# Layer norm ahead of a feed-forward block: GpSimd's eight residual products are held until VectorE has corrected the first results, and ScalarE's copies of them are spread over the block

## The reference

```python
def layer_norm(x, g, b):
    mu = jnp.mean(x32, axis=-1, keepdims=True)
    var = jnp.mean(jnp.square(x32 - mu), axis=-1, keepdims=True)
    return ((x32 - mu) * lax.rsqrt(var + LN_EPS) * g + b)

def swiglu(h, w_gate, w_up, w_down):
    return (jax.nn.silu(h @ w_gate) * (h @ w_up)) @ w_down

for i in range(2):
    ...
    x = layer_norm(ALPHA * x + (1.0 + g_m) * y, ln_mix_g[i], ln_mix_b[i])
    h = x * (1.0 + sc_f) + sh_f
    y = swiglu(h, w_gate[i], w_up[i], w_down[i])
    x = layer_norm(ALPHA * x + (1.0 + g_f) * y, ln_ffn_g[i], ln_ffn_b[i])
```

## Time and profile before

| | us |
|---|---|
| median of 3 runs (lowest, highest) | 1160.9 (1159.54, 1163.73) |
| the profiled execution, whole | 1165.62 |
| its span, first to last instruction | 1164.3 |
| TensorE busy | 1132.3 (97%) |
| VectorE busy | 839.1 (72%) |
| ScalarE busy | 628.7 (54%) |
| GpSimd busy | 77.8 (7%) |

### The profile page before, as it was taken

The page is one execution under the profiler, slowest core; times in us unless marked ns, Lnnn a source line. Parts: engine busy times, 40 slices in busy tenths (PEclk is TensorE's granted clock), DMA queues, the critical chain, the costliest instruction groups (busy, mean ns, idle before and its releaser), DMA issues.

```text
span 1164.3 us, 24996 instructions
## 1 busy us (share of the span) xinstructions
PE 1132.3 (97%) x10542; PEld 1083.9 (93%) x10542; DVE 839.1 (72%) x1427; ACT 628.7 (54%) x1075; POOL 77.8 (7%) x101
## 2 busy tenths in 40 slices
PE   7999989999999999989999999999999999999998
PEld 6997779999998999989999999999999999999987
DVE  5699579888885788797566569768656667676743
ACT  3477447444443677666444454744654557565542
POOL 3000012000000200120000004400000000000000
PEclk9999999999999999999999999999999999999999
DMA  9963756988997544546646552754245554656550
GB/s 321 378 222 125 274 182 218 310 300 273 341 304 262 199 146 146 182 146 216 217 152 208 186 181 73 236 164 147 74 146 182 178 179 132 200 177 204 183 179 37
DMA packets 194687, 232.22 MB, mean 199 GB/s; under 512 B 4083, under 2 KB 169555, under 8 KB 194576
## 3 DMA queue, kind: packets, MB, share of 16 engines
q1 hardware_dynamic: 193984, 230.32, 59.5%
q0 software_dynamic: 592, 0.31, 0.2%
HBM read 229.56 MB, written 1.05 MB: 198 GB/s over the span
## 4 chain that ended last, share of the span: by engine, by line
PE 85%; DVE 8%; DMA 2%; issue 2%; ACT 1%; SPq 1%; POOL 0%; DVEq 0%; ACTq 0%
PE ps L154 84%; DVE wlo L187 2%; DMA raw<-in_w_in_even_dram 2%; PE ps L157 2%; DVE hL L196 1%; DVE T L187 1%; DMA MW<-in_w_mod_dram 1%; SPq L224 1%; DVE first L187 1%; DVE LT L196 1%; DVE LT L187 1%; DVE Fg L196 0%; ACT whi L166 0%; DVE T L196 0%; POOL T L187 0%
## 5 line engine op out<-in xcount | busy, mean ns | idle before, releaser
L187 DVE TENSOR_TENSOR wlo<-raw,whi 128x1024 fp32r<-128x1024 f32 (+1 forms) x346 | 408.7, 1202 | 165.4 <-ACT whi L166 163.0
L154 PE MATMUL ps<-hH,whi 128*128 128x256 f32 (+3 forms) x1792 | 516.9, 288 | 1.5 <-DVE hL L196 1.1
L154 PE MATMUL ps<-hH,wlo 128*128 128x256 f32 (+3 forms) x1792 | 505.8, 282 | 6.1 <-DVE wlo L187 6.1
L154 PE MATMUL ps<-hL,whi 128*128 128x256 f32 (+3 forms) x1792 | 505.7, 282 | 0.0
L166 ACT ACTIVATE whi<-raw 128x1024 fp32r<-128x1024 f32 (+1 forms) x346 | 349.8, 1033 | 198.9 <-PE ps L154 136.5
L154 PEld LDWEIGHTS ps<-hH,whi 128*128 128x128 f32 x1792 | 338.8, 189 | 7.2 <-issue 3.8
L154 PEld LDWEIGHTS ps<-hH,wlo 128*128 128x128 f32 x1792 | 338.9, 189 | 7.1 <-DVE wlo L187 7.1
L154 PEld LDWEIGHTS ps<-hL,whi 128*128 128x128 f32 x1792 | 339.3, 189 | 0.3
L154 PE MATMUL ps<-uL,whi 128*128 128x256 f32 x352 | 99.2, 282 | 0.0
L154 PE MATMUL ps<-uH,whi 128*128 128x256 f32 x352 | 99.0, 281 | 0.0
L154 PE MATMUL ps<-uH,wlo 128*128 128x256 f32 x352 | 98.4, 279 | 0.0
(11 more groups left out here) (314 smaller groups left out, 1618.3 us busy)
## 6 DMA issues: line engine op xcount, KB each, us to landing
MW<-in_w_mod_dram SPq DMA_DIRECT2D x47, 1024.0 KB, 6.3
raw<-in_w_up_dram SPq DMA_DIRECT2D x44, 1024.0 KB, 5.6
raw<-in_w_in_dram SPq DMA_DIRECT2D x36, 1024.0 KB, 5.0
raw<-in_w_down_dram SPq DMA_DIRECT2D x27, 1024.0 KB, 5.8
raw<-in_w_gate_dram SPq DMA_DIRECT2D x22, 1024.0 KB, 7.2
raw<-in_w_in_odd_dram SPq DMA_DIRECT2D x12, 1024.0 KB, 5.4
raw<-in_w_in_even_dram SPq DMA_DIRECT2D x8, 1024.0 KB, 9.6
raw<-in_w_down_dram SPq DMA_DIRECT2D x8, 768.0 KB, 6.9
```

Source lines behind the costliest of these rows:

```text
L154: return self.queued(self.e.matmul(out, lhsT, rhs, start=start, stop=stop, skip_group_check=True, **kw), length if pos is None else max(le ...
L187: return self.queued(self.e.tensor_tensor(out, a, b, op), 0.07 + cols(out) / self.RATE)
```

## The change

GpSimd gets a second wait, for `k.raw_done`, ahead of its eight products, where the norm is one that runs ahead of a feed-forward block (`early` with `to`). Each product and its copy are now emitted at least 2 us of modelled TensorE time after the one before. `gated` waits for less: steps 0 and 1 for `raw_done` alone, step 2 also for the last `hL`, step 3 also for the last copy to XA. Steps 2 and 3 swap their pieces of `LT`, so that the piece with `rstd` is used last.

```diff
@@ layer_norm @@
     k.hold = False
+    if early and to is not None:
+        while k.raw_done is None:
+            yield None
+        pool.wait_ge(*k.raw_done)
     for i in range(0, KD, 2):
         if to is not None:
             for j in (i, i + 1):
+                if early:
+                    yield k.pe.clock + 2.0
                 t = pool.tt(T(j), T(j), rstd, ALU.mult).inc()
                 yield due(t)
                 new[j] = act.wait_ge(*t).act(X(j), T(j), ACT.Identity, scale=ag[:, j:j + 1], bias=ab[:, j:j + 1]).inc()
@@ gated @@
-    sg = m.l4[s % 4]
+    sg = m.l4[(0, 1, 3, 2)[s % 4]]
     if s == 0:
         f = m.first
         c = yield from normalized(k, y, f)
-    while not k.normed or k.raw_done is None:
+    while k.raw_done is None or s == 3 and not k.normed:
         yield None
     yield due(y, k.raw_done)
     act.wait_ge(*y)
     if s == 0:
         act.table(SET_SILU)
     if s < 4:
-        for mark in (*k.normed, k.raw_done):
-            act.wait_ge(*mark)
+        act.wait_ge(*k.raw_done)
+        if s > 1:
+            act.wait_ge(*k.h_low[KD - 1])
+        if s > 2:
+            act.wait_ge(*k.normed[0])
     else:
         act.wait_ge(*k.u_low[2 * s - 8])
```

## The result

The change brings 1158.04 us (median of 18 runs, 1155.35 to 1162.43) against 1162.97 us for the kernel before in the same session (18 runs, 1159.54 to 1165.23). The ratio is 0.9963 with a 95% interval of 0.9953 to 0.9973. That is 4.3 us (3.1 to 5.5) less, where 6.5 were forecast; the ratio compares means, and the two medians are 4.9 apart. The three earlier runs of before had a median of 1160.9, 2.1 us lower than the 18, so the forecast of 1154.4 is 3.6 too low (2.1 from the base, 1.6 from the gain in medians), inside its range of 1151.5 to 1160.0. The gain lies under the 0.5% that the prediction asks for to call a kernel faster, although its interval excludes zero.

What follows compares the result with a forecast made beforehand. TensorE, busy for 97% of the span, was taken as the bound, losing time at two places to late weight residues. Gains of 3.0 + 3.6 = 6.6 us, rounded to 6.5, gave 1154.4 us, range 1151.5 to 1160.0.

Steps and rivals of the forecast that it cites:

- The cause: VectorE's four products `first` x `rstd` take turns with GpSimd's eight, 0.90 us each against 0.34 alone, making weight residues late.
- The first place: TensorE's gap near 194 us: 3.3 us lost including low clock, 0.3 would remain, gain 3.0 us.
- The second place: TensorE's gap near 522 us: 4.4 us lost including low clock, 0.8 would remain, gain 3.6 us.
- the row at 699.50: Two residues in a row took 2.35 us while GpSimd's product waited; taken as nearer, so 0 delay between first two residues.
- The row at 384.94: One residue beside GpSimd took 1.74 us against 1.2 alone, 0.54 more for each; the other bound.
- The rule of the port: VectorE operations with two SBUF inputs share GpSimd's port lock, so delay moves to residues; sum 6.0 instead of 6.6 us.
- The clock: Full clock stays at both places after the change, returning 1.4 and 1.5 us; stretch 166 to 170 cited as support.
- Rival A: Clock stays low at one place, 1.5 us stay, or late up-weight DMA gives the same time: 1155.9 us; chance 0.17.
- The copies and `gated`: ScalarE's copies holding step 3's high parts cost 0; shorter waits in `gated`, with SiLU about 2 us earlier, gain 0.
- rival D: ScalarE's copies wait for products and hold step 3's high parts: 3.1 us lost per place, 1164.1 us; chance 0.05.
- Given back: TensorE comes sooner to weights bounded by DMA or buffer, nothing is left of the gain: 1160.9 us; chance 0.10.
- Rival B: Turns go on between residues, step 3's first residues late too; about 3 us of gain left, 1157.9 us; chance 0.10.

Runs made afterwards that it cites:

- Experiment 1: The changed kernel without GpSimd's second wait, the rest of the change kept, against the kernel before: ratio 1.0001, 1163.35 us.
- 5: The changed kernel without the wait and with the eight residual products on VectorE instead of GpSimd: ratio to the kernel before 0.9948, 1156.71 us.
- 7: The changed kernel with the eight residual products left out, each copy taking the unscaled sum: ratio to the kernel before 0.9946, 1156.69 us.
- experiment 8: The kernel before, unchanged, profiled once more: one run, 1162.27 us.
- experiment 9: The changed kernel, unaltered, profiled and timed once more against the kernel before: ratio 0.9964, 1157.72 us against 1162.32.
- experiment 3: The changed kernel with GpSimd waiting for the third residue instead of `raw_done`: ratio to the kernel before 0.9966, 1159.38 us.
- experiment 2: The kernel before with only GpSimd's wait for `raw_done` added, `gated` still waiting for all eight copies: ratio 1.0009, 1164.66 us.
- 4: The changed kernel with two residues put ahead of VectorE's four products `first` x `rstd`: ratio to the kernel before 0.9948, 1157.04 us.

## Why the prediction was right, and where it was off

- **The cause.** Right. GpSimd's products made VectorE's four late, and parting them gave 1.43 us for four (forecast 1.34). Experiment 1 shows that the whole gain hangs on this wait, and 5 and 7, with GpSimd out of the way, show the residues at 1.14 us again.
- **The first place.** The sum had 3.0. The profiled pair gives 2.06 - 0.35 - 0.32 (the modulation wait, not foreseen) + 1.4 of clock = 2.8. That agrees, but two of its terms don't hold in every execution: the clock loss (1.4) is missing behind this gap in experiment 8, and what is left is 0.33 + 0.85 instead of 0.35 when the weights are early, with 0.44 for the modulation (9). The place is worth between 2.06 - 1.18 - 0.44 = 0.4 and 2.8 us, and I had added the upper end in full. That the first profiled pair came so near 3.0 is in part luck.
- **The second place.** The sum had 3.6, with 0 for GpSimd's turn between the first two residues. This step failed. It was 0.54: remaining 0.59 + 0.85 = 1.44, which is the other bound (1.4) to the tenth, and the gain is 4.37 - 1.44 = 2.9. Experiments 3 and 7, with no product there, leave 0.87, near the 0.8 that I took. I had chosen the row at 699.50 as the nearer, where two residues passed a waiting product. The row at 384.94, 1.74 for one residue, was the one that held.
- **The rule of the port.** Rows first: three kinds of VectorE operations with two inputs from SBUF are delayed at the second place beside GpSimd, the residues (1.68 against 1.14 apart), `LT<-first,ST,LT` (1.84 for two against 0.88 in experiment 3) and `uL` (1.22 for one against 0.68 before). The first residue there, which was already running, was not, nor were the two at 699.50, where GpSimd's product was the one held back. The four that also read PSUM, `first<-LT,ST,ps`, took 1.66 us in both profiles, beside GpSimd in the one and alone in the other. The Trainium skill ("SBUF — State Buffer", section "SBUF: two separate sides") says this of operations with two SBUF inputs, and the trace agrees. By that rule the prediction gave 6.0 us, and the profiled pair has 5.7 to 5.9.
- **The clock.** Right for what remains: 1.00 over both places, in both profiles of the change, with 0.35 to 1.44 us left in pieces. The reason given for it doesn't hold: behind the stretch at 166 to 170, which stayed at 1.00 in the first profile, experiment 8 has half clock. And what the change gives back of the clock was taken too high, 1.4 + 1.5 = 2.9. In the session of experiment 9, three runs of before and seven of the change have the same mean granted clock, 0.998. They took 1160.7 and 1157.6 on average, 3.1 us apart, where the sum without the clock has 1.6 + 2.1 = 3.7. The two medians of the session are 4.6 apart, so only about 1.5 us are left for the clock (an estimate: the clock is known to 0.001, about a microsecond). Rival A did not come, nor its late DMA as a loss: the late weights made the turn harmless.
- **The copies and `gated`.** The value 0 for the shorter waits was right for them alone (1) and wrong as a description. Together with the spread copies they carry everything once the wait is there, since without them it costs as much as it brings (2). The price of rival D was put at eight copies held ahead of step 3. The wait alone does that, and it measured 1.8 us a place against 3.1 forecast; one reason is that the eight products take 10.47 us there, 1.3 each and not 1.74.
- **Given back.** Not at these places. The stretches between fixed points (the first matmul of T with ones in each norm) shrank by 2.9 us in the first layer and 2.9 in the second, and by 0.2, -0.1 and 0 elsewhere. The part ahead of them was 1.1 longer, which leaves the 4.8 us between the two profiled executions. The later pair (8 and 9) differs by 0.1 us ahead of them, and shrank by 2.4 and 2.9; of that 2.4 some 1.5 is the half clock at 167 to 170, ahead of the changed part. Between the two layers 9 took 1.4 longer, with half clock at 371 that 8 hasn't.
- **The sum.** 2.8 + 2.9 = 5.7 where the profile has all terms, 0.4 + 2.9 = 3.3 where the first place has little. The measured 4.3 (3.1 to 5.5) lies between, and the forecast of 6.5 above. It also lies below the 5.5 to 7.3 that the prediction gives for its own case; its parts add up to 6.0 to 6.9, and no term is given for the ends 5.5 and 7.3.
- **Rival B.** Half of its mechanism came. The turns do go on at the residues (its first sign, 1.7 in a row), but they open no gap at step 3 (its second), so they cost 0.54 us at the second place and up to that at the first, and not the 3.5 us of the rival. That the measured 1158.04 is next to its 1157.9 is chance: the base was 2.1 higher than assumed.

## What to carry to other kernels

When a helper engine and the main one get in each other's way, moving the helper's work moves the collision. Look at what the main engine does next, and put the turns on work that nobody waits for yet. A later start may need other queues to be loosened before it pays: each half of this change was worth nothing alone. A loss that hangs on the clock behind a gap should be counted in full only where several profiles show it, and a stretch that kept its clock in one profile is no proof that it always does.

## What the runs showed of the hardware

- **Two engines take turns, a whole instruction at a time, where both have work.** At the second place after the change, VectorE's second and third residues take 1.76 us each, and GpSimd's eight products take 1.41 each on average, against 0.82 before. Two rows of GpSimd's timeline there: the first product, which starts inside the first residue (519.58 to 520.80) and ends 0.58 after it, and the next two, 1.7 each beside residues of 1.7:

```profile
519.80 1.58 POOL L187 TENSOR_TENSOR T<-T,LT 128x256 f32<-128x256 f32 x1 [25.24 <-DVE first L187]
...
521.35 3.40 POOL L187 TENSOR_TENSOR T<-T,LT 128x256 f32<-128x256 f32 x2
```

- Why the product at 699.33 in the earlier trace rows was passed by two residues, when this one was passed by none, stays open.
- **The same gap may or may not cost the clock.** 1.7 + 0.3 us of gaps were followed by 20 matmuls in 3.5 us in one execution and by 28 in another of the same kernel. In experiment 2 two gaps of 0.9 us were followed by the full clock at one place and by 0.50 at the other, in one execution. What decides it, the runs don't show. Over the runs the time follows the mean granted clock: of the 30 runs of before beside experiments 1 to 4, the 8 with 0.995 took 1163.4 us on average and the 4 with 0.998 took 1160.8. The median clock is 0.995 there (0.991 to 0.998) and 0.998 for the change (18 runs, 0.995 to 0.999).
